# Second feed-forward part of a two-block fp32 layer: high weights times both halves of the activations in one 512-column matmul

## What is computed

```python
def conv_gated_mlp(h, w_up, conv_w, conv_b, w_down):
    gate, up = jnp.split(h @ w_up, 2, axis=-1)
    return (jax.nn.gelu(dwconv_centred(gate, conv_w, conv_b), approximate=True) * up) @ w_down

x = x + g2 * conv_gated_mlp(modulate(rmsnorm(x, norm2_g[l]), sh2, sc2), *ffn)
return rmsnorm(x, final_norm_g)
```

## Time and profile before

| | |
|---|---|
| median of 3 runs | 2571.61 us (2571.49 to 2571.88) |
| span of the profiled execution | 2574.2 us, 2.6 us (0.1%) above that median |
| work around the span | the span runs from the first to the last instruction; nothing is counted outside it |
| granted TensorE clock, mean of the span | 0.999 of full |
| PE busy | 2547.2 us, 20808 matmuls |
| DVE busy | 1930.3 us, 75% |
| ACT busy | 1186.6 us, 46% |
| second feed-forward part on PE | from 1836.35 us to some 2557.9 us |

### The profile page before, as it was taken

The page is one execution under the profiler, slowest core; times in us unless marked ns, Lnnn a source line. Parts: engine busy times, 40 slices in busy tenths (PEclk is TensorE's granted clock), DMA queues, the critical chain, the costliest instruction groups (busy, mean ns, idle before and its releaser), DMA issues.

```text
span 2574.2 us, 49638 instructions
## 1 busy us (share of the span) xinstructions
PE 2547.2 (99%) x20808; PEld 2468.1 (96%) x20808; DVE 1930.3 (75%) x2468; ACT 1186.6 (46%) x1263; POOL 0.2 (0%) x4
## 2 busy tenths in 40 slices
PE   9999999999999999999999999999999999999997
PEld 9889999999999999999999899959999999999997
DVE  8888887997999888888893236787666666666667
ACT  7766564444544444444443234443544444444443
POOL 0000000000000000000000000000000000000000
PEclk9999999999999999999999999999999999999999
DMA  8766667767888888888763344424455555555552
GB/s 310 254 245 213 226 241 253 246 238 247 294 281 289 286 283 288 286 282 286 269 247 99 99 164 149 153 81 164 164 191 190 193 197 196 190 190 195 197 193 103
DMA packets 282441, 558.10 MB, mean 217 GB/s; under 512 B 10295, under 2 KB 16728, under 8 KB 281944
## 3 DMA queue, kind: packets, MB, share of 16 engines
q1 hardware_dynamic: 282120, 553.47, 63.1%
q10 hardware_dynamic: 144, 2.10, 0.2%
HBM read 553.43 MB, written 2.10 MB: 216 GB/s over the span
## 4 chain that ended last, share of the span: by engine, by line
PE 92%; DVE 4%; DMA 1%; ACT 1%; issue 1%; SPq 0%; DVEq 0%; ACTq 0%
PE PS L1766 80%; PE PS L1777 3%; PE PS L1780 3%; PE PS L1779 3%; DVE WL L956 1%; DMA adab<-in_ada_w 1%; PE PS L2098 1%; PE PS L2013 1%; DMA X<-in_x 0%; DVE ada1c L1215 0%; DVE SQ L982 0%; DVE X L1334 0%; PE PS L2045 0%; PE PS L2108 0%; PE PS L2023 0%
## 5 line engine op out<-in xcount | busy, mean ns | idle before, releaser
L515 ACT ACTIVATE WH<-RAW 128x1024 fp32r<-128x1024 f32 x840 | 887.6, 1060 | 1249.2 <-PE PS L1766 1123.2
L956 DVE TENSOR_TENSOR WL<-RAW,WH 128x1024 fp32r<-128x1024 f32 x840 | 1017.2, 1222 | 569.8 <-ACT WH L515 560.2
L1766 PE MATMUL PS<-XL,WH 128*128 128x256 f32 x4288 | 664.5, 277 | 0.0
L1766 PE MATMUL PS<-XH,WH 128*128 128x256 f32 x3752 | 586.3, 278 | 1.8 <-ACT WH L515 1.1
L1766 PEld LDWEIGHTS PS<-XL,WH 128*128 128x128 f32 x4288 | 569.3, 188 | 0.0
L1766 PE MATMUL PS<-XH,WL 128*128 128x256 f32 x3752 | 503.4, 277 | 0.0
L1766 PEld LDWEIGHTS PS<-XH,WH 128*128 128x128 f32 x3752 | 498.5, 188 | 4.2 <-issue 2.5
L1766 PEld LDWEIGHTS PS<-XH,WL 128*128 128x128 f32 x3752 | 461.6, 188 | 0.0
L1766 PE MATMUL PS<-HH,WH 128*128 128x256 f32 x1728 | 268.2, 277 | 3.3 <-DVE X L1334 2.7
L1766 PE MATMUL PS<-HL,WH 128*128 128x256 f32 x1728 | 266.1, 276 | 0.0
L1766 PEld LDWEIGHTS PS<-HH,WH 128*128 128x128 f32 x1728 | 228.3, 188 | 4.1 <-DVE X L1334 3.1
(11 more groups left out here) (284 smaller groups left out, 1890.1 us busy)
## 6 DMA issues: line engine op xcount, KB each, us to landing
RAW<-in_w_ff SPq DMA_DIRECT2D x128, 1024.0 KB, 6.0
RAW<-in_w_in SPq DMA_DIRECT2D x111, 1024.0 KB, 5.0
RAW<-in_w_up SPq DMA_DIRECT2D x88, 1024.0 KB, 4.9
adab<-in_ada_w SPq DMA_DIRECT2D x128, 512.0 KB, 5.4
RAW<-in_w_down SPq DMA_DIRECT2D x44, 1024.0 KB, 5.0
ada1b<-in_ada_w SPq DMA_DIRECT2D x64, 512.0 KB, 6.0
RAW<-in_w_out SPq DMA_DIRECT2D x32, 1024.0 KB, 5.1
RAW<-in_w_oa SPq DMA_DIRECT2D x8, 1024.0 KB, 5.2
```

What stands on the lines that cost most here:

```text
L515: A(WH[:, c.base % 2, hs], RAW[:, c.base % SLOTS, hs], ACT.Copy).then_inc(hi_done, 1)
L956: tt(WL[:, b, hs], RAW[:, c.base % SLOTS, hs], WH[:, b, hs].bitcast(f32), ALU.subtract)\
L1766: ins = MM(out[:, f, :], w[:, b, kk, f * P:(f + 1) * P], x, start=first and not low and n == 0 and f % 2 == 0, stop=last and low, skip_gro ...
```

## The change

In the second feed-forward part alone, the high and the low activations of a k tile become one moving operand of 2 x 256 columns. `two` issues one matmul of 512 columns with `WH`, whose output is a whole PSUM bank (first half: high, second half: low), and one of 256 columns with `WL`, which adds to the second half. The sum of the halves is made when the product is read. To let one access pattern reach both halves, `XH` and `XL` (and `HH`, `HL`, `MH`, `ML`, `CH`, `CL`) become the two rows of one tensor, at the addresses they had, and the first two k tiles of the low half get a place beside those of the high half. In all other parts PE keeps the three matmuls of 256 columns, or `tok`. A product of this part now takes four banks, so that the two slots fill PSUM; the last norm's sums move from bank 4 to bank 0 and wait for that slot.

```diff
-SUM_BANK = [4, 4, 4, 7, 1, 0, 6, 4, 4]
+SUM_BANK = [4, 4, 4, 7, 1, 0, 6, 4, 0]
...
+        XP = at("XP", [P, 2, KC, T], 80 * K + 192, f32r)
+        XH, XL = XP[:, 0], XP[:, 1]
+        FIRST_ROW = 4 * K + 40
+        XP_FIRST = at("XP_FIRST", [P, 2, FIRST_ROW], 80 * K + 32, f32r)
...
+        def both_of(pair, k):
+            return XP_FIRST[:, :, k * T:(k + 1) * T] if k < 2 and pair is XP else pair[:, :, k, :]
...
+        def acc_two(s):
+            return PS[:, 4 * s:4 * s + 4, :].rearrange("p f (m t) -> p m f t", t=T)
...
-                A(GS[:, :, :], acc_ws(q.slot), ACT.Copy).then_inc(acc_free[q.slot], 1)
+                A(GS[:, :, :], acc_two(q.slot)[:, 1], ACT.Copy).then_inc(sm["gate_low"], 1)
+
+            def hidden_up(c, q, j):
+                done(c)
+                if j.since(1):
+                    act.wait_ge(sm["gated"], j.value())
+                A(FR[:, :, :], acc_two(q.slot)[:, 1], ACT.Copy).then_inc(sm["up_low"], 1)
...
+                    if s == 9:
+                        hidden_up(c.plus(7), q.plus(1), j.plus(1))
...
                     V.tensor_copy(cw[:, :], src).then_inc(sm["cw_done"], 1)
+                    dve.wait_ge(sm["gate_low"], j.value(1, 1))
+                    tt(GS[:, :, :], acc_two(q.slot)[:, 0], GS[:, :, :], ALU.add).then_inc(acc_free[q.slot], 1)
                     dve.wait_ge(acc_free[q.slot], q.turns(2, 1))
...
-            def gated(q, c, j):
-                done(c)
+            def gated(q, j):
+                dve.wait_ge(sm["up_low"], j.value(1, 1))
+                tt(FR[:, :, :], acc_two(q.slot)[:, 0], FR[:, :, :], ALU.add).then_inc(acc_free[q.slot], 1)
                 dve.wait_ge(sm["gelu_done"], j.value(1, 1))
                 dve.wait_ge(sm["hid_lo"], j.value(1, STEPS1))
-                tt(FQ[:, :, :], acc_ws(q.slot), CV[:, :, :], ALU.mult).then_inc(acc_free[q.slot], 1)
+                dve.wait_ge(acc_free[q.slot], q.turns(2, 1))
+                tt(FQ[:, :, :], FR[:, :, :], CV[:, :, :], ALU.mult).then_inc(sm["gated"], 1)
...
             def down_out2(q, c, s, last=False):
                 done(c)
-                for k in range(4):
-                    ins = stt(X[:, 4 * s + k, :], acc_ws(q.slot)[:, k, :], mod[:, 5 * KC + 4 * s + k, 0:1],
-                              X[:, 4 * s + k, :], ALU.mult, ALU.add)
-                    if last and k < 3:
-                        ins.then_inc(sm["last_x"], 1)
+                for m in (1, 0):
+                    for k in range(4):
+                        ins = stt(X[:, 4 * s + k, :], acc_two(q.slot)[:, m, k, :], mod[:, 5 * KC + 4 * s + k, 0:1],
+                                  X[:, 4 * s + k, :], ALU.mult, ALU.add)
+                        if m:
+                            own.did(ins)
+                        elif last and k < 3:
+                            ins.then_inc(sm["last_x"], 1)
+                    if m:
+                        own.settle()
                 ins.then_inc(acc_free[q.slot], 1)
...
+            def two(out, c, x, first, last, kk, low):
+                b = c.base % 2
+                for f in (0, 2, 1, 3):
+                    w = (WL if low else WH)[:, b, kk, f * P:(f + 1) * P]
+                    if low:
+                        ins = MM(out[:, 1, f, :], w, x[:, 0, :], start=False, stop=last, skip_group_check=True)
+                    else:
+                        ins = MM(out[:, :, f, :], w, x, start=first, stop=False, skip_group_check=True)
+                return ins
...
-                    wide(c.plus(s), q, s)
+                    wide(c.plus(s), q, s, two)
...
-                    wide(c.plus(4 + s), q.plus(1), s)
+                    wide(c.plus(4 + s), q.plus(1), s, two)
...
-                    down(c.plus(8 + s), q.plus(2 + s), j, s, STEPS1)
+                    down(c.plus(8 + s), q.plus(2 + s), j, s, STEPS1, two)
...
+            last = Place(Q_END - 2)
+            pe.wait_ge(acc_free[last.slot], last.turns(2, 1))
             norm_sum(N_LAST, SQ)
```

More of the change, by code:

```diff
@@ L175, in build_program @@
         X = at("X", [P, KC, T], 64 * K)
[L176 to L180, removed]
+        XP = at("XP", [P, 2, KC, T], 80 * K + 192, f32r)
+        XH, XL = XP[:, 0], XP[:, 1]
+        FIRST_ROW = 4 * K + 40
+        XP_FIRST = at("XP_FIRST", [P, 2, FIRST_ROW], 80 * K + 32, f32r)
+        XH_FIRST, XL_FIRST = (XP_FIRST[:, m, 0:2 * T].rearrange("p (k t) -> p k t", t=T) for m in range(2))
+        HP = at("HP", [P, 2, 2, FT, T], 112 * K + 192, f32r)
+        HH, HL = HP[:, 0], HP[:, 1]
         NT = at("NT", [P, KC, T], 112 * K + 192)
@@ L204, in parts_of @@
                 return [(rest, slice(0, 4))]
[L205 removed]
+            return [(XH_FIRST if x is XH else XL_FIRST, slice(0, 2)), (rest[:, 2:4, :], slice(2, 4))]
         def tile_of(x, k):
[L209 removed]
+            if k < 2 and (x is XH or x is XL):
+                return (XH_FIRST if x is XH else XL_FIRST)[:, k, :]
+            return x[:, k, :]
+        def both_of(pair, k):
+            return XP_FIRST[:, :, k * T:(k + 1) * T] if k < 2 and pair is XP else pair[:, :, k, :]
         def col(name, n=0, w=1):
@@ L920, in ff2_step @@
                         gate_gelu(Place(0))
+                    if first and s == 1:
+                        hidden_up(c.plus(-1), q.plus(-1), Place(0))
                     if first and s == 2:
-                        hidden_high2(q.plus(-1), Place(0))
+                        hidden_high2(Place(0))
                     if s == 5:
@@ L1759, in use, with ws @@
                     pe.wait_ge(acc_free[q.slot], q.turns(2))
-            def ws(out, c, xh, xl, first, last, kk, low):
+            def ws(out, c, x, first, last, kk, low):
                 b = c.base % 2
-                for n, (w, x) in enumerate(((WL, xh),) if low else ((WH, xh), (WH, xl))):
+                for n, w in enumerate((WL,) if low else (WH, WH)):
                     for f in (0, 2, 1, 3):
-                        ins = MM(out[:, f, :], w[:, b, kk, f * P:(f + 1) * P], x,
+                        ins = MM(out[:, f, :], w[:, b, kk, f * P:(f + 1) * P], x[:, n, :],
                                  start=first and not low and n == 0 and f % 2 == 0, stop=last and low,
@@ L1769, in ws, with tok @@
                 return ins
-            def tok(out, c, xh, xl, first, last, kk, low):
+            def two(out, c, x, first, last, kk, low):
[7 more added lines that the diff above has]
+                return ins
+            def tok(out, c, x, first, last, kk, low):
                 b = c.base % 2
                 for t in range(TT):
-                    h, l = xh[:, t * P:(t + 1) * P], xl[:, t * P:(t + 1) * P]
+                    h, l = x[:, 0, t * P:(t + 1) * P], x[:, 1, t * P:(t + 1) * P]
                     if low:
@@ L1781, in tok, with product @@
                 return ins
-            def product(c, q, s, xh, xl, k0=0, first=True, last=True, fn=ws, out=None, e=None):
+            def product(c, q, s, pair, k0=0, first=True, last=True, fn=ws, out=None, e=None):
                 if q is not None and first:
@@ L1793, in product @@
                 if out is None:
-                    out = (acc_ws if fn is ws else acc_as)(q.slot)
+                    out = {ws: acc_ws, two: acc_two, tok: acc_as}[fn](q.slot)
                 for h in range(2):
@@ L1802, in product, with wide, down @@
                         for kk in range(HF * h, HF * h + HF):
-                            ins = fn(out, c, tile_of(xh, k0 + kk), tile_of(xl, k0 + kk), first and kk == 0,
-                                     last and kk == FT - 1, kk, low)
+                            ins = fn(out, c, both_of(pair, k0 + kk), first and kk == 0, last and kk == FT - 1, kk, low)
                     ins.then_inc(pe_half, 1)
-            def wide(c, q, s, fn=ws, e=None, xh=XH, xl=XL):
-                product(c, q, s, xh, xl, 4 * s, s == 0, s == SLOTS - 1, fn, e=e)
-            def down(c, q, j, s, before=0):
+            def wide(c, q, s, fn=ws, e=None, pair=XP):
+                product(c, q, s, pair, 4 * s, s == 0, s == SLOTS - 1, fn, e=e)
+            def down(c, q, j, s, before=0, fn=ws):
                 if s == 0:
                     pe.wait_ge(sm["hid_lo"], j.value(1, before + 1))
-                product(c, q, s, HH[:, j.base % 2], HL[:, j.base % 2])
+                product(c, q, s, HP[:, :, j.base % 2], fn=fn)
             def first_columns(c):
@@ L1930, in _ @@
                     norm_sum(N_FF1, NT, [0])
-                wide(Place(C_OUT1 + t), Place(Q_OUT1 + t // 4), t % 4, e=E_OUT1, xh=MH, xl=ML)
+                wide(Place(C_OUT1 + t), Place(Q_OUT1 + t // 4), t % 4, e=E_OUT1, pair=MP)
             def sum_columns(a):
@@ L1988, in beside_context @@
                             k = 4 * s + kk
-                            fn(out, c, CH[:, k, :], CL[:, k, :], k == 0, k == KC - 1, kk, low)
+                            fn(out, c, CP[:, :, k, :], k == 0, k == KC - 1, kk, low)
             def attention2_step(t):
```

28 lines of the change are left out of this document (14 added, 14 removed).

## The result

| | before | after |
|---|---|---|
| median of 4 runs | 2571.55 us (2571.03 to 2571.88) | 2607.07 us (2606.58 to 2608.57) |
| ratio | | 1.0136, 95% interval 1.0124 to 1.0148 |
| span of the profiled execution | 2574.2 us | 2605.8 us |
| second feed-forward part to the end of the span | 737.85 us | 773.01 us |

The change costs 35.5 us, 1.4%. The prediction said 2601 us, slower, with a range of 2582 to 2616. The spans differ by only 31.6 us. The changed kernel's profiled execution has a time of 2607.56 us, 1.8 more than its span; with the same 1.8, the profiled execution of before took 2576.0, 4.4 us over its median, and not 2.6 as the text ahead has it. The excess lies ahead of the change: the part starts at 1836.35 us there and at 1832.79 here.

What follows compares the result with a forecast made beforehand. PE's pace was taken to bound the part. Pace +4.0 us, DVE's second passes +16.9 us over nine steps and +8.5 us at the end made 29.4 us on 2571.6: 2601 us, range 2582 to 2616.

Steps and rivals of the forecast that it cites:

- On this trace a long matmul saves nothing: PE's merged matmuls: 512 columns, at 229.2 ns in `tok`, take no less than twice the 113.3 ns of 256.
- The first rival: Merged matmuls on PE pay their fixed part once: 2580 us at 215.8 ns, 2586.5 us at 220; chance 0.22.
- I take 229.2: Pace in ns of PE's merged matmul, from `tok` rows, against 226.7 for the replaced pair: +4.0 us.
- The bound of 235 ns: Upper bound for one merged matmul on PE: 2.5% over `tok`'s row, for its second run of columns.
- the second rival: On PE, merged matmuls take 235 ns and 256-column ones 4 ns more: +19.3 us, in all 2616 us; chance 0.14.
- How many chunks feel this pace: PE's pace counts in 98 of 132 chunks: first 8, plus 8 wide and first down chunk per step; 1568 merged matmuls.
- 1.9 us late per step: After the down chunks, DVE's second passes delay the next gate product by 1.9 us, in nine steps: +16.9 us.
- The end, +8.5 us: From the tenth step's down chunks through the last four chunks, DVE's second passes delay the last pass's end by 8.5 us.
- What follows it is as before: Behind the last pass over the last four chunks, everything up to the span's end runs unchanged, with no added time.
- What would show it: Profile signs: long matmuls 229 ns apart, PE idle near 0.4 and 1.8 us at L1723, steps 67.7 instead of 65.5 us.
- What costs nothing: DVE's additions for gate and up products, SP's loads, the four banks and new addresses add nothing on the path.
- The sum: Over the whole kernel, 4.0 + 16.9 + 8.5 = 29.4 us on 2571.6 us: 2601 us, 1.1% slower.

Runs made afterwards that it cites:

- 5: Changed kernel with the long matmuls, except the four that start each product's accumulation, cut to 384 columns (2 x 192): 2521.85 us.
- 2: Changed kernel with DVE's second pass over the down products left out, so their high half misses `X`: 2584.66 us, ratio 1.0051 to the kernel before.
- 4: Changed kernel with long matmuls reading two neighbouring k tiles of the high activations, 512 contiguous columns, low activations left out: 2606.79 us, ratio 1.0137.
- Experiment 1: Changed kernel without the merge: three matmuls of 256 columns, still four banks and two DVE passes over down products: 2597.94 us, ratio 1.0108 to before.
- 7: Changed kernel with four extra fp32 matmuls into a free bank after each of the last norm's first two sums: 2606.06 us, ratio 1.013 to before.
- 6: Changed kernel with this part's low-weight matmuls also made 512 columns long, so every matmul there is long: 2835.41 us.
- 8: Changed kernel with blocks of weights and PSUM banks both taken in order 0, 1, 2, 3 instead of 0, 2, 1, 3: 2607.68 us, ratio 1.0138.
- 9: Changed kernel with weight blocks in order 0, 1, 2, 3 but banks written in order 0, 2, 1, 3: 2607.32 us.

## Why the prediction was right, point by point

- **"On this trace a long matmul saves nothing"**: right. 232.5 ns in the rows above, 173.4 at 384 columns (5), and +13.5 us for the merge alone (2). The first rival, a fixed part paid once (215.8 or 220 ns), had 0.22 and falls. The Trainium skill (TensorE: Matmul & The Clock Gate, Back-to-back issue gap) has 216 ns for a single matmul of 512 columns and 131 ns for a sustained stream. For fp32r the trace agrees with neither: 232.7 ns, at a granted clock of 1.00 in the paced stretches.
- **"I take 229.2"**: this is the term that was mis-sized. The ten paced stretches cost 9.5 us, not 4.0. Nine of them hold 0.11 us each, in all 1.0, that belong to the next point: the slower first run after a wait. The other 8.5 us are, over 10 x 144 long matmuls, 5.9 ns each over the pair of 226.7, which is 232.6. The row of `tok` was near, as the prediction said, but not the same (over 840 starts of `tok` in the trace of before, without the eleven of 314 ns and more, the mean is 229.3), and 3.4 ns on 1440 matmuls is 4.9 us. The bound of 235 ns took this in; its reason, a second run of columns, was wrong (4). Of the 4 ns that the second rival put on each short matmul less than 1 came: 0.91 us for eight is 114 ns each, against 113.3.
- **"How many chunks feel this pace"**: 98 were counted. The first eight gave only 0.1 us instead of 0.3: in the kernel before, the half chunks of the first gate product took 2.83 to 2.93 us there, not 2.72, and now they take 2.77 to 2.91, so that this product became 0.3 us shorter and the up product behind it 0.4 longer. Why the first one is slow is open. The others did as counted.
- **"1.9 us late per step"**: right in its chain of times. From the start of the first pass to that of the gate product it was 2082.14 - 2066.52 = 15.62 us, predicted 2013.97 - 1998.20 = 15.77. The 0.12 us that PE loses after a restart was put ahead of the gate product; it showed behind it. 15.6 us in nine steps and the 1.0 us just named stand against 16.9. Experiment 1 shows that a PE faster by 0.1 us a chunk does not shorten the 18.05.
- **"The end, +8.5 us"**: 1.8 + 6.8 = 8.6.
- **"What follows it is as before"**: wrong by 1.4 us. The step that failed is that a last pass that is late moves everything behind it unchanged. The later passes left PE with gaps of 1.1 to 1.8 us between the sums, and the granted clock fell to 0.50 while the last sums were on the path (7).
- **"What would show it"**: the waits on line 1723 came, but the step is 68.2 us, not 67.7, and the sign of 1.8 us of idle time before the gate product was misworked. By the prediction's own times PE would have been ready at 2007.15 + 5.44 = 2012.59 and waited 1.3 us. The trace lists 0.82 there and nothing before c+10. By the starts above, c+9 takes 5.83 us and c+11 6.53, where a chunk without a wait takes 5.55: 0.3 and 1.0 us late.
- **"What costs nothing"**: held for the gate and up products. With the second passes on the down products gone and both of these left in, only the pace of PE remained (2), and the part had no other new wait.
- **The sum**: 29.4 us predicted, 35.2 between the traces and 35.5 between the medians. Of the 5.8 us missing between the traces, 4.6 are pace (8.5 + 0.1 against 4.0) and 1.4 the clock; the steps gave 16.6 against 16.9, the end 8.6 against 8.5. The mechanism, DVE's second passes ahead of the slot, was right. The pace was not within the forecast's own bounds: 232.7 ns lies outside its 226 to 232, and 2607.07 us outside its 2597 to 2606. What took the result in was the range, whose upper end comes from the second rival and its wrong reason, and that part is luck.

## What to carry to other kernels

Before two matmuls are merged into one, look up in the kernel's own trace whether the time goes with the columns or with the instructions: here it went with the columns, so a third fewer instructions bought nothing, and the merge by itself cost 13.5 us. A sum that PSUM made for nothing costs a pass of DVE for each product when its halves are kept apart, and the place to price it is the tightest stretch of that engine, walked row by row up to the moment at which the slot is wanted. A few ns on an instruction that occurs 1,500 times is as large a term as a visible wait, so the pace should be taken from a row with the same operand as stationary, or carry its own margin.

## What the runs showed of the hardware that was not expected

- An fp32r matmul takes 0.448, 0.452 and 0.454 ns a column at 256, 384 and 512 columns (114.7, 173.4 and 232.7 ns): the steps from 256 to 384 to 512 leave no fixed part at all.
- With the weights stationary, starts of 512-column matmuls in a steady stream are mostly 236 and 231 ns apart in turn (6), and in a run of eight behind shorter ones 226, then 236 and 231 in turn, whatever the order of banks and blocks (8, 9); with the weights moving, in `tok`, the mean is 229.2.
- A matmul stream that restarts after a wait on a read of PSUM starts 0.05 us after the read's end and takes 0.11 us more for its first eight long matmuls.
- At the end of the program PE stood still for 1.1, 1.7 and 1.8 us, with two sum instructions between one gap and the next, and the granted clock then read 0.57 and 0.50; with eight fp32 instructions in each of the last two gaps it read 1.00. Behind a single gap of 1.86 us before the last eight sums (6) it also read 1.00, and they took 1.99 us.
